# Sparse attention in a 16-step software pipeline: two score groups moved ahead of transposes on TensorE, one coefficient moved ahead on VectorE

## The reference

```python
s_s = einsum(q, k_sel) * scale ; p_s = masked_softmax(s_s) ; o_s = p_s @ v_sel
s_w = einsum(q, k_win) * scale ; p_w = masked_softmax(s_w) ; o_w = p_w @ v_win
o_c = masked_softmax(q @ kc.T * scale) @ vc        # 31 compressed keys
return gc[..., 0:1] * o_c + gc[..., 1:2] * o_s + gc[..., 2:3] * o_w
```

## Time and profile before

| what | value |
|---|---|
| median of 3 runs | 2719.41 us (2719.03 to 2721.03) |
| the profiled execution: its time | 2721.04 us |
| the profiled execution: its span, first to last instruction | 2719.7 us |
| TensorE busy | 2629.8 us, 97% of the span |
| VectorE, ScalarE, GpSimd busy | 33%, 34%, 47% |
| mean granted TensorE clock | 0.979 of full |
| the 16 steps of the attention, first turn to last product | 648.26 to 849.4 us |

### The profile page before, as it was taken

One profiled execution on the slowest core, in us unless ns is written; L12 is line 12 of the kernel. 1 busy time (PEld: TensorE's weight loads), 2 busy tenths in 40 slices (PEclk: granted clock), 3 DMA queues, 4 the chain that ended last, 5 costly groups with the idle time before them and its releaser, 6 DMA issues.

```text
span 2719.7 us, 30088 instructions
## 1 busy us (share of the span) xinstructions
PE 2629.8 (97%) x12030; PEld 2114.7 (78%) x12030; DVE 906.8 (33%) x1513; ACT 931.4 (34%) x1505; POOL 1276.7 (47%) x641
## 2 busy tenths in 40 slices
PE   8999999998999999999999999998988899899998
PEld 7888888866666788888887888887876688788886
DVE  4222111186665213344313455203036522311101
ACT  4223221225554323322323222223257532322221
POOL 4444444537774444444444444444444344444443
PEclk9999999999999999999998999997998999799999
DMA  4322322412001323455432555331320033132321
GB/s 161 101 94 95 93 91 88 140 40 78 1 1 39 101 95 95 133 186 186 145 93 68 174 186 186 112 93 47 108 84 8 32 98 97 55 100 94 97 93 58
DMA packets 87339, 261.50 MB, mean 96 GB/s; under 512 B 10528, under 2 KB 11808, under 8 KB 87200
## 3 DMA queue, kind: packets, MB, share of 16 engines
q1 hardware_dynamic: 83888, 255.46, 28.7%
q10 hardware_dynamic: 3312, 4.12, 0.5%
HBM read 257.44 MB, written 2.10 MB: 95 GB/s over the span
## 4 chain that ended last, share of the span: by engine, by line
PE 90%; DVE 4%; POOL 3%; ACT 2%; issue 1%; DMA 0%; SPq 0%; DVEq 0%; ACTq 0%
PE ps L283 80%; POOL prob L1731 3%; PE ps L294 2%; PE ps L1539 1%; PE ps L1509 1%; PE ps L925 1%; PE ps L1007 1%; PE ps L319 0%; PE ps L1496 0%; PE ps L1875 0%; PE ps L1497 0%; PE ps L932 0%; PE ps L1546 0%; PE ps L2080 0%; POOL split_ring L270 0%
## 5 line engine op out<-in xcount | busy, mean ns | idle before, releaser
L270 POOL TENSOR_TENSOR split_ring<-raw_ring,split_ring 128x1024 fp32r<-128x1024 f32 x416 | 1018.9, 2453 | 1170.6 <-ACT split_ring L263 1170.4
L283 PE MATMUL ps<-hs,split_ring 128*128 128x512 f32 x6048 | 1395.4, 392 | 16.4 <-DVE hs L373 9.2
L283 PEld LDWEIGHTS ps<-hs,split_ring 128*128 128x128 f32 x6048 | 1139.5, 189 | 261.0 <-issue 12.4
L263 ACT ACTIVATE split_ring<-raw_ring 128x1024 fp32r<-128x1024 f32 x416 | 436.5, 1051 | 419.0 <-PE ps L283 406.0
L283 PE MATMUL ps<-ffn_act,split_ring 128*128 128x512 f32 x2112 | 495.4, 396 | 0.0
L283 PEld LDWEIGHTS ps<-ffn_act,split_ring 128*128 128x128 f32 x2112 | 397.8, 188 | 97.0
L569 ACT ACTIVATE ffn_act<-tmp 128x512 fp32r<-128x512 f32 x88 | 55.6, 632 | 395.9 <-DVE tmp L607 395.9
L1731 POOL TENSOR_SCALAR prob<-prob,small 128x512 f32<-128x512 f32 (+3 forms) x128 | 140.9, 1121 | 50.7 <-DVE small L1769 50.7
L607 DVE TENSOR_TENSOR tmp<-ps,tmp 128x512 f32<-128x512 f32 x44 | 30.4, 691 | 304.9 <-PE ps L283 304.9
L283 PE MATMUL ps<-split_ring,hs 128*128 128x512 f32 (+1 forms) x480 | 102.2, 374 | 0.0
L283 PEld LDWEIGHTS ps<-split_ring,hs 128*128 128x128 f32 x480 | 85.3, 188 | 15.9 <-issue 1.0
(11 more groups left out here) (346 smaller groups left out, 2540.7 us busy)
## 6 DMA issues: line engine op xcount, KB each, us to landing
raw_ring<-in_wstream SPq DMA_DIRECT2D x380, 512.0 KB, 3.5
ada_w<-in_w_ada SPq DMA_DIRECT2D x96, 256.0 KB, 3.7
raw_ring<-in_wstream SPq DMA_DIRECT2D x32, 384.0 KB, 3.1
sq<-in_w_ada SPq DMA_DIRECT2D x48, 256.0 KB, 3.7
x<-in_x_t SPq DMA_DIRECT2D x4, 512.0 KB, 6.2
decay<-in_decay ACTq DMA_DIRECT2D x8, 256.0 KB, 2.7
out_t<-x SPq DMA_DIRECT2D x8, 256.0 KB, 2.0
raw_ring<-in_wstream SPq DMA_DIRECT2D x4, 304.0 KB, 2.7
```

Of the source, the lines that this page charges most:

```text
L263: nc.scalar.activation(self.split[:, s, 0, :], self.raw[:, s, :], ACT.Copy).then_inc(self.sem("unit_hi"), 1)
L270: nc.gpsimd.tensor_tensor(self.split[:, s, 1, :], self.raw[:, s, :], self.split[:, s, 0, :].bitcast(F32), ALU.subtract).then_inc(self.sem( ...
L283: mm = self.nc.tensor.matmul(out, lhs, rhs, start=first and j == 0, stop=last and j == 2)
```

## The change

TensorE: the scores of banks 3 and 4 of the next step are no longer issued behind the turn of bank 4; those of bank 3 go ahead of the turn of bank 3, those of bank 4 ahead of the turn of bank 4. The product with the values stays where it was. VectorE: part 0 of the coefficients of the next step goes from behind the maxima of banks 2 and 3 to ahead of them, right behind the copy of turn 3 (and so ahead of `dve_q_rope` in even bodies). No instruction is added or taken away, and none of ScalarE, GpSimd or the DMA queues is moved.

```diff
@@ pe_nsa
             if g == 0 and t < 7:
                 self.pe_make_q(t + 1)
+            if ahead:
+                self.pe_n_scores(p + 1, 3)
             self.pe_n_turn(p, 3)
             if g == 0:
                 self.pe_cmp_turn(t)
+            if ahead:
+                self.pe_n_scores(p + 1, 4)
             self.pe_n_turn(p, 4)
-            if ahead:
-                self.pe_n_scores(p + 1, 3)
-                self.pe_n_scores(p + 1, 4)
             if g == 1 and t < 7:
                 self.pe_cmp_scores(t + 1)
             self.pe_n_values(p)
@@ dve_nsa
             self.dve_n_turned(p, 3)
+            if ahead:
+                self.dve_n_coef(p + 1, 0)
             if g == 0 and t < 7:
                 self.dve_q_rope(t + 1)
             if ahead:
                 self.dve_n_maxima(p + 1, 1)
-                self.dve_n_coef(p + 1, 0)
                 self.dve_n_maxima(p + 1, 2)
```

## The result

The changed kernel takes 2703.81 us (median of 4 runs, 2702.3 to 2703.93) against 2720.2 for the kernel before on the same chip: 16.4 us less, ratio 0.9939 with a 95% interval of 0.9922 to 0.9956. The forecast was 2705.2 in a range of 2702 to 2711. The profiled execution has a span of 2702.5 us, 17.2 less than in the earlier trace rows.

A forecast was written before the change was run, and what follows sets the result against it. The loop through GpSimd's scaling was taken as the bound, TensorE's order next at 23.25 us a pair. Seven pairs at 1.85 (12.95) plus 1.3 at the end gave 14.25 us off 2719.4: 2705.2, range 2702 to 2711.

The forecast's parts named there:

- What bounds: Attention's loop of last scaling, turn 4, scores 3 and 4, maxima, coefficients part 0, next scaling; 25.13 us a pair.
- The odd body: Odd-numbered attention bodies, in seven repeating pairs: end at +10.99 instead of +11.92, 0.93 us less each.
- The even body: Even-numbered attention bodies, in seven repeating pairs: end at +12.25 instead of +13.22, 0.97 us less each.
- The tie with GpSimd: Odd body's turn 4: GpSimd's scaling allows it at +17.53, TensorE reaches it at +17.38; 0.05 us charged per pair.
- The end: From body 14 to step 15's values: they start at +16.46 instead of 17.78, saving 1.3 us.
- The clock: Last values, 5.90 instead of 4.46 us at granted clock 0.76: up to 1.44 us might return; kept for the range.
- The middle coefficients: Rival, chance 0.12: GpSimd late in every pair, part 1 0.5 to 1 us later in even bodies; 2708.7 to 2712.
- Only the end gains: Rival, chance 0.06: moved scores 3 and 4 cost as much as the waits they fill; 1.3 us left, 2718.
- Slower: Rival, chance 0.05: turn 3 issued 0.8 us later holds copies back; part 1 2.9 us late gives 2726.
- The lock: Rival, chance 0.05: even body's rotation waits at most 1.6 us for GpSimd's first scaling operation; 8.8 us lost, 2714.

The follow-up runs named there:

- Each half alone: TensorE's reordering with VectorE's order as before: 2705.07 us; VectorE's earlier part 0 with TensorE's order as before: 2712.56 us.
- the extra operation: Changed kernel plus one GpSimd operation (256 columns times 1.0) ahead of the last of eight in steps 1 to 14: 2706.58 us.
- two variants: TensorE's reordering alone, VectorE as before: 2705.07 us; changed kernel with one extra GpSimd operation in step 15 alone: 2703.96 us.

## Why the prediction was right

**What bounds.** Right. The loop of last scaling, turn 4, scores, maxima, part 0, next scaling was the bound, with TensorE next. Each half alone shows it.

**The odd body.** Forecast +5.13 for turn 4, +6.53 for the values, 10.99 in all; measured +5.09, +6.47 and 10.93. GpSimd's start was forecast at +5.75 and came at 737.01 - 731.28 = +5.73. The copy of turn 4 was just in time, as reckoned. GpSimd's gap for part 1 was put at 0.7 us and is 0.48.

**The even body.** Forecast +6.35, +7.79 and 12.25; measured +6.26, +7.74 and 12.19. GpSimd's start was put at +6.67 and came at +6.57. Turn 3 came 0.09 earlier than reckoned (+4.81), the compressed turn took 0.14 instead of 0.23 us, and turn 4 then lost 0.09 again to VectorE's copy of turn 3. The copy had been put at +6.30 against +6.35 for the turn, "no wait to speak of"; it ended at +6.20, with TensorE ready at about +6.14.

**The tie with GpSimd.** Here the terms were too dear. Part 1 was to be done at +11.66 and the scaling at +17.39; GpSimd resumed at 730.31 - 719.09 = +11.22 and ended at +16.65. The 2.70 us from bank 2's exponential to part 1 came from an odd body, where compressed work of VectorE lay in between, and its multiply was the one of 0.45 us beside GpSimd; after the change it finds GpSimd waiting for it and takes 0.17. The six operations took 5.43, not 5.65. So there was no tie but 0.5 us of slack, which the extra operation measured as 0.49, and the 0.05 us that I charged a pair was 0. A pair saves 2.01 us, not 1.85: 0.05 of that is the tie, the rest the two bodies' 0.06 each. Over seven pairs it is 1.1 us of the miss. The sign that scalings would start 23.2 to 23.4 us apart was missed by as little: 23.11 (725.66 to 748.77).

**The end.** 1.3 us forecast, 1.5 measured.

**The clock.** The 1.44 us that I left out and kept in the range came back whole, 1.4 us, in each of two executions of the changed kernel and in all of its variants with a stretch up to 5.85 us. The stretch did get shorter, 4.91 us where I had forecast 5.2, but that reason is not enough: 5.59 and 5.85 us did no harm in two variants. The forecast's sum with this term would have been 15.7; with the pairs' 1.1 and the end's 0.2 it is 17.0, against 16.4 in the medians and 17.1 in the traces. All three errors lie on the same side, so none hid another; the time looks closer (2703.81 for 2705.2) than the saving (16.4 for 14.2) because the forecast started from 2719.4, and the kernel before had a median of 2720.2 with its fourth run.

**The rivals.** The middle coefficients did not rule: the gaps for part 1 exist (1.16 and 0.48 us) and are covered. Only the end gains: no. Slower: no, the copies that come later are still in time. The lock: VectorE and GpSimd do hold each other, by 0.39 us for the first two scaling operations beside the rotation (3.49 and 3.10 us), and `dve_split_q` took 1.51 instead of 1.39 us. The rotation itself stayed at 0.69. The rival had the order wrong by the forecast's own starts: the rotation at +6.55 is ahead of GpSimd at +6.67, so that the rotation had nothing to wait for, and its 1.6 us was not seen. The rule of the Trainium skill, "SBUF — State Buffer", section "Who interferes with whom", that the later of the two is blocked until the earlier is done, goes with the 0.39: the rotation started at 725.48, GpSimd at 725.66, and GpSimd was the one held; a block up to the rotation's end would have been 0.51 us. It does not go with the split, which began inside GpSimd's first two operations and lost 0.12 us only (0.34 in the variant with part 0 behind the rotation, where it took 1.73).

## What to carry to other kernels

When a hand-ordered queue waits for another engine, look behind the waiting instruction for work whose own inputs are long there, and put it in front: here twelve matmuls in front of two turns filled three waits and were worth 15 of 16.4 us. Price such a wait by the starts of the instructions around it and not by the idle time shown: 1.40 us of idle time were 2.0 us of a pair. Two edits that break the same loop don't add up (15.2 and 7.7 give 16.4); cost each alone, and count the waits that only one of them cures. A stall that another engine gets inside its own work is free as long as its last result is in time; measure that slack by adding one operation of known length.

## What the runs showed that I had not expected

The granted clock fell ahead of the last values of the kernel before in three executions of three (5.9, 6.0, 6.9 us for 16 products instead of 4.45), though the stretch ahead of them, with much waiting of TensorE, was just 5.66 us in the first of them, and TensorE was busy for 3.0 of it. It stayed at full speed behind 4.91 us in the changed kernel and behind 5.59 and 5.85 us in two variants. The fall came 4.3 to 6.1 us into the stretch. How long TensorE had little to do doesn't settle it alone. What else does stays open, and so does whether the changed kernel's 4.91 us are always short enough: two executions are all that were traced.

And a small multiply of VectorE on 4 columns (L1769, part 1) took 0.33 or 0.45 us beside GpSimd's scaling, and 0.17 when GpSimd was standing. Being beside it is not enough, though: the one on 2 columns (part 2) took 0.16 beside it, before and after. Two 512-column operations beside it took 1.39, 1.51 or 1.73 us, a loss of at most 0.34.
